# Moving a state-space set-up out of the first projection and into the first MLP of a three-layer network on one core

## The reference, cut to what matters

```python
def first_block(...):                       # layers 0 and 1
    h = concatenate([meta, x])              # 528 x 1024
    for i in range(2):
        hn = rmsnorm(h, norm_attn[i])
        h = h + (even_mixer if i == 0 else odd_mixer)(hn, ...)
        h = h + (relu(rmsnorm(h, norm_mlp[i]) @ w_up[i]) ** 2) @ w_down[i]

def even_mixer(h, ...):
    qa, ka, va, qb, kb, vb = split(h @ w_in)         # 18 tiles of 128 columns
    oa = differential attention(qa, ka, va, bias = table[bucket(k - q)])
    qb, kb = rmsnorm(qb), rmsnorm(kb)                # per head of 64
    qb, kb = axial_rope(qb), axial_rope(kb)
    ob = dense attention(qb, kb, vb)
    return concat(oa, ob) @ w_out

def odd_mixer(h, ...):                               # window of 128, bias by the same table, a sink column
    ...

def s5_ssm(u, a, log_dt, b, c, d_skip):              # in layer 2, which also has attention and an FFN
    dt = exp(log_dt); bar = exp(a * dt)              # complex, 32 groups x 64 states
    bb = (bar - 1) / a * b                           # 32 x 64 x 16
    h_t = bar * h_(t-1) + bb @ u_t ; y_t = Re(c @ h_t) + d_skip * u_t
```

## Time and profile before

| | us |
|---|---|
| time, median of 3 runs (2389.45 to 2392.06) | 2391.89 |
| the profiled execution, its own time | 2387.33 |
| its span | 2385.5 |
| PE busy | 2218.0 (93%) |
| PE weight loads busy | 1864.6 (78%) |
| DVE, ACT, POOL busy | 1173.1 (49%), 785.0 (33%), 884.8 (37%) |

### The profile page before, as it was taken

One profiled execution on the slowest core, in us unless ns is written; L12 is line 12 of the kernel. 1 busy time (PEld: TensorE's weight loads), 2 busy tenths in 40 slices (PEclk: granted clock), 3 DMA queues, 4 the chain that ended last, 5 costly groups with the idle time before them and its releaser, 6 DMA issues.

```text
span 2385.5 us, 33836 instructions
## 1 busy us (share of the span) xinstructions
PE 2218.0 (93%) x13234; PEld 1864.6 (78%) x13234; DVE 1173.1 (49%) x1732; ACT 785.0 (33%) x1271; POOL 884.8 (37%) x384
## 2 busy tenths in 40 slices
PE   3596979999999999999999998999999999999996
PEld 2595757999999976787888877778867788887875
DVE  4666765651253326564045346857654554443224
ACT  2122655331222236432122323234332332222223
POOL 0231024444444434444444433323333444444442
PEclk9797989999999999999999999999989999999998
DMA  5753000333333350133333354323222333332321
GB/s 139 144 187 68 1 1 20 90 96 89 88 95 91 88 168 2 46 96 93 92 97 90 95 141 114 115 64 91 78 73 69 93 104 90 97 92 86 97 85 54
DMA packets 371761, 209.93 MB, mean 88 GB/s; under 512 B 25935, under 2 KB 362928, under 8 KB 370752
## 3 DMA queue, kind: packets, MB, share of 16 engines
q1 hardware_dynamic: 353088, 184.21, 26.8%
q10 hardware_dynamic: 18560, 24.13, 4.4%
HBM read 196.85 MB, written 15.41 MB: 89 GB/s over the span
## 4 chain that ended last, share of the span: by engine, by line
issue 40%; PE 32%; POOL 18%; DVE 5%; ACTq 2%; ACT 2%; DMA 1%; POOLq 0%; SPq 0%; DVEq 0%
POOL w_lo L731 17%; PE acc L799 8%; PE acc L800 8%; PE acc L801 8%; PE acc L875 2%; PE ops L904 2%; ACTq L1353 2%; PE tps L893 1%; DVE probs L1929 1%; ACT probs L1370 1%; PE ops L891 1%; POOL probs L754 1%; DVE root L2269 1%; PE tps L858 0%; ACT probsT L1386 0%
## 5 line engine op out<-in xcount | busy, mean ns | idle before, releaser
L731 POOL TENSOR_TENSOR w_lo<-raw,w_hi 128x1024 fp32r<-128x1024 f32 x328 | 804.1, 2451 | 1256.1 <-ACT w_hi L1257 1241.2
L1257 ACT ACTIVATE w_hi<-raw 128x1024 fp32r<-128x1024 f32 x327 | 346.7, 1060 | 1132.5 <-PE acc L801 1064.2
L799 PE MATMUL acc<-hr_hi,w_hi 128*128 128x512 f32 x1120 | 450.2, 402 | 6.7 <-DVE u_t L2419 5.5
L800 PE MATMUL acc<-hr_lo,w_hi 128*128 128x512 f32 x1120 | 445.1, 397 | 0.0
L801 PE MATMUL acc<-hr_hi,w_lo 128*128 128x512 f32 x1120 | 445.1, 397 | 0.0
L799 PE MATMUL acc<-hn_hi,w_hi 128*128 128x264 f32 (+1 forms) x896 | 265.9, 297 | 39.2 <-POOL w_lo L731 35.0
L800 PE MATMUL acc<-hn_lo,w_hi 128*128 128x264 f32 (+1 forms) x896 | 263.2, 294 | 0.0
L801 PE MATMUL acc<-hn_hi,w_lo 128*128 128x264 f32 (+1 forms) x896 | 262.8, 293 | 0.0
L799 PEld LDWEIGHTS acc<-hr_hi,w_hi 128*128 128x128 f32 x1120 | 211.9, 189 | 63.5 <-issue 7.0
L801 PEld LDWEIGHTS acc<-hr_hi,w_lo 128*128 128x128 f32 x1120 | 211.8, 189 | 51.5
L800 PEld LDWEIGHTS acc<-hr_lo,w_hi 128*128 128x128 f32 x1120 | 212.1, 189 | 50.2 <-issue 0.7
(11 more groups left out here) (370 smaller groups left out, 3747.9 us busy)
## 6 DMA issues: line engine op xcount, KB each, us to landing
raw<-in_w_up SPq DMA_DIRECT2D x64, 512.0 KB, 4.0
raw<-in_w_down SPq DMA_DIRECT2D x64, 512.0 KB, 3.8
raw<-in_w_in SPq DMA_DIRECT2D x56, 512.0 KB, 3.8
raw<-in_w_ffn_gate SPq DMA_DIRECT2D x22, 512.0 KB, 3.8
raw<-in_w_ffn_up SPq DMA_DIRECT2D x22, 512.0 KB, 3.8
raw<-in_w_in_even SPq DMA_DIRECT2D x18, 512.0 KB, 7.6
raw<-in_w_ffn_down SPq DMA_DIRECT2D x16, 512.0 KB, 3.8
bias_c<-bias_c_d SPq DMA_DIRECT2D x1, 5392.0 KB, 17.7
```

Of the source, the lines that this page charges most:

```text
L731: nc.gpsimd.tensor_tensor(w_lo[:, part], raw[:, slot], w_hi[:, part].bitcast(F32), ALU.subtract).then_inc(sems["lo"], T.up("lo"))
L799: mm(out, w_hi[:, part, w0 + k, :], xh, start=s0, stop=False)
L800: mm(out, w_hi[:, part, w0 + k, :], xl, start=False, stop=False)
L1257: fn(w_hi[:, n % 2], raw[:, n % 4], ACT.Copy).then_inc(sems["hi"], T.up("hi"))
```

## The change

- **Start.** `x` and the meta tokens are SP's first loads; the ten small loads are issued by ACT. The squares are summed by PE with a matrix of ones (L959 of the changed file) as they come, in place of DVE's additions.
- **State-space set-up.** All of it leaves the start and `even_in`. Its loads are issued by SP in `even_out` (`ssm_loads`), after a clearing of `rows2` that DVE does behind attention B. DVE does the arithmetic in pieces, one after each tile of `up00`, `down00` and `up01` (`next(setup)`), the big products in halves of 1024 numbers; PE transposes the parameters in `up00` and does `kernel_products` and `turn_powers` in `down00`; the products by `c` overwrite `pw_re` and `pw_im`, so they wait for `turn_powers`. `up00` and `down00` are unrolled.
- **Bias tables.** ACT issues only `bias_a_d` at the start. The band part of the other table is spread by SP (`bands_d`, eight DMAs in `up00`); its 17 leading columns are made by 32 small products on PE (`lead_products`). SP loads the table in the middle of `odd_q`, in three DMAs, not after it.
- **Heads.** Order of `even_in`: the six tiles of the B part, the four of A's values, then queries and keys in turn. The norms of the heads are done after tiles 1 to 5, SP sends `rot_e` behind its load of tile 11, DVE rotates one head after each of tiles 9 to 13, and the values are transposed after tiles 6 to 10.

The products stand behind a tile's own work, never ahead of the taking of its accumulator. The diff, cut to its core:

```diff
@@ SP
-            for r0, v in ((0, a["norm_attn"]...
-                load(rows[r0:r0 + v.shape[0], :], v, "vec_in")
-            load(ident[:], a["c_ident"], "vec_in")
-            load(meta_in[:], a["meta_tokens"], "x_in")
             for t in range(4):
                 load(xin[:, t, :], a["x"][0, t * P:(t + 1) * P, :], "x_in")
+            load(meta_in[:], a["meta_tokens"], "x_in")
...
+            def spread_bands(n):
+                hs, at, w = 4 * (n // 2), (0, 3 * P)[n % 2], (3 * P, 2 * P)[n % 2]
+                load(bands_d[hs:hs + 4, :, at:at + w], bass.AP(band_d.tensor, ...), "bands_out")
...
+            def bias_c_load(first):
+                if first:
+                    T.saw("rstd", 3)
+                    sp.wait_ge(sems["rstd"], T.at("rstd"))
+                    sp.wait_ge(sems["lead_out"], T.at("lead_out"))
+                    sp.wait_ge(sems["bands_out"], T.at("bands_out"))
+                    load(lead_o[:].rearrange("p x h m -> p (x h m)"), lead_d, "bias_in")
+                at, c, w = (BAND_W, 3 * P, 2 * P) if first else (0, 0, 3 * P)
+                load(bias_c[:, :, at + LEAD_2:at + LEAD_2 + w], bands_d[:, :, c:c + w]..., "bias_in")
-            units(even_in, {3: setup_loads, 14: mixer_loads})
-            units(even_out)
+            units(even_in, {3: setup_loads, 11: swap_heads, 12: bias_a_load})
+            units(even_out, {4: ssm_loads})
-                units(by_name[f"up0{half}"])
+                units(by_name[f"up0{half}"], {} if half else {2 + n: lambda n=n: spread_bands(n) for n in range(8)})
-            units(odd_q)
-            load(bias_c[:], bias_c_d.rearrange("h p c -> p h c"), "bias_in")
+            units(odd_q, {2: lambda: bias_c_load(True), 3: lambda: bias_c_load(False)})
@@ PE
-            project(even_in, None, H_LO, first_stats, after={
-                6: kernel_products, **{7 + n: lambda n=n: turn_powers(n) for n in range(4)},
-                **{11 + n: head_sums(n) for n in range(5)}})
-            tokens_first(qkv_e, (8, 9, 10, 11, 17))
+            project(even_in, None, H_LO, None, after={
+                0: bias_products, 1: head_sums(0), 2: after_third, 3: head_sums(2), 4: head_sums(3), 5: head_sums(4),
+                **{6 + n: lambda v=v: value_tokens(v) for n, v in enumerate((17, 8, 9, 10, 11))}})
...
+                turns = {1: lambda: turn_parameters(0), 2: lambda: turn_parameters(1)}
+                tables = {2: kernel_products, **{3 + n: lambda n=n: turn_powers(n) for n in range(4)}}
+                project(by_name[f"up{i}0"], None, H_LO, (first_stats, second_stats)[i], {} if i else turns)
+                project(by_name[f"down{i}0"], None, ("hidden_lo", MLP_HALF), None, {} if i else tables)
@@ ACT
-            for at, q0, w0, w in ((0, N_META + P, P - 1, 3 * P), (BAND_W, N_META, 2 * P - 1, 2 * P)):
-                dma(bias_c_d[:, :, at:at + LEAD_2], bass.AP(bias_d.tensor, ...), "bias_c_out")
-                dma(bias_c_d[:, :, at + LEAD_2:at + LEAD_2 + w], bass.AP(band_d.tensor, ...), "bias_c_out")
@@ DVE, in mlp(0)
+                        if i == 0 and isinstance(m, int):
+                            next(setup, None)
```

More of the change, by code:

```diff
@@ new lines, in bias_products, with lead_products @@
+            def bias_products():
+                T.saw("consts", 64)
+                pe.wait_ge(sems["consts"], T.at("consts"))
+                for c in range(0, N_REL, 512):
+                    n = min(512, N_REL - c)
+                    b = open_("t_")
+                    close(mm(tps[b][0:20, 0:n], table[:], onehot[:, c:c + n], start=True, stop=True), b, "t_")
+            def lead_products():
+                T.saw("bias_rows", 2)
+                pe.wait_ge(sems["bias_rows"], T.at("bias_rows"))
+                b = open_("t_")
+                for x, q0 in enumerate((N_META + P, N_META)):
+                    for m in range(N_META):
+                        at = q0 - m - 1
+                        c = (x * N_META + m) * 16
+                        ins = mm(tps[b][:, c:c + 16], bias_back[:, at:at + P], ident[0:20, 4:20], start=True, stop=True)
+                close(ins, b, "t_")
@@ new lines, in _ @@
+                fn(hn_hi[:, k, :], h[:, k, :], ACT.Copy, scale=gains[:, k:k + 1]).then_inc(sems["h_hi"], T.up("h_hi"))
+                if k > 1:
+                    T.saw("summed")
+                    act.wait_ge(sems["summed"], T.at("summed"))
+                fn(sq[:, k % 2, :], h[:, k, :], ACT.Square).then_inc(sems["square"], T.up("square"))
+                if k == 4:
+                    T.saw("raw0", 16)
+                    act.wait_ge(sems["raw0"], T.at("raw0"))
+                    fn(w_hi[:, 0], raw[:, 0], ACT.Copy).then_inc(sems["hi"], T.up("hi"))
@@ L1499, in _ @@
[L1499 to L1506 removed]
+                if m == 0:
+                    for _ in range(3):
+                        others(T, "t_")
+                if m == 1:
+                    T.saw("bias_rows", 2)
+                    act.wait_ge(sems["bias_rows"], T.at("bias_rows"))
+                    dma(bias_d, bias_row[:], "bias_out")
+                    dma(band_d, band_row[:], "bias_out")
@@ L1547, in _ @@
+            mlp(0, parameters, tables, store_ca)
+            act.wait_ge(sems["ssm_out"], T.at("ssm_out"))
             project(odd_kv, first=first_stats)
```

659 lines of the change are left out of this document (371 added, 288 removed).

## The result

| | before | after |
|---|---|---|
| time, median (range, 4 runs each) | 2390.67 (2388.72 to 2392.06) | 2347.01 (2346.19 to 2351.95) |
| profiled execution, own time; its span | 2387.33; 2385.5 | 2347.00; 2345.1 |
| ratio after / before, 95% interval | | 0.9822 [0.9805, 0.9839] |
| PE busy; mean granted clock | 2218.0; 0.967 | 2232.4; 0.974 |

The account below looks back on a forecast made before the run. PE bounds the kernel except in two nearly idle stretches, up to 79.3 and 230.7 us. Terms: 80.5 + 2 - 15.1 - 1 - 2 = 64.4 us gained, giving 2327.5 against the median 2391.9; range 2315 to 2345.

Parts of the forecast that it names:

- the chain behind the last tile: After even_in's last tile at 204.6: heads normed, rot_e sent, five heads rotated, first attention A scores only at 230.70.
- Slower and no change: Slower, 0.01: PE stays at its lower level after kernel_products; no change, within some 5 us: 0.01.
- The start: Before even_in: x issued first, h copies from about 10.4 us, first even_in product at 29.5, bounds 27.5 and 33.
- lead_products: In even_in: 32 small products on PE, taken at 4.6 us, bounds 3.6 and 5.3.
- The set-up on DVE lies beside PE: In up00 and down00: DVE's set-up hides, up to 4 us behind where PE's next accumulator has 5.8.
- set-up is not hidden: Rival, up00 to up01: 14 units with large products each lose 1.5 us, 21 in all, so 2348; chance 0.12.
- The danger on POOL: In the MLP: DVE products lengthen POOL's w_lo to up to 3.6 us; cost 1, bounds 0 and 6.
- kernel_products: In the MLP: 10.6 us added on PE, part of 15.1 together with turn_powers and parameter transposes.
- Bands on SP: In up00: 5.24 MB on SP between weight loads, against three units of reserve; cost nothing, bound 8.
- odd_q: In odd_q: bias_c between the weight loads makes unit 4 arrive late; 2 us lost, bounds 0 and 6.
- Attention: After the first scores: PE that hasn't stood and an exponential table already loaded gain 2 us, bounds 1 and 3.
- Heads within the projection: In even_in: ACT and DVE keep pace with head norms, and rot_e's DMAs hold SP 6.7 us; both cost nothing.

Follow-up runs that it names:

- run 11: The kernel before, with the four bias_c_d DMAs issued by SP behind its fourth load of even_out, not by ACT at the start: 2359.1 us, 0.9878.
- Run 8: The changed kernel with the identity as SP's first load and bias_c loaded behind all loads of odd_q: 2341.3 us, 0.9789 to the kernel before.
- run 9: The changed kernel with all 64 kernel_products reading rows 0 to 63 instead of alternating halves: 2364.3 us, 0.9879 to the kernel before.
- runs 10 and 11: The kernel before with bias_c_d's DMAs issued by SP: first behind its even_in loads, 2366.0 us; then behind its fourth even_out load, 2359.1 us.
- run 12: The changed kernel with leading columns by DMA, bias_c behind odd_q's loads, kernel_products in four groups and the set-up laid out anew: 2313.3 us, 0.9670.
- run 4: The changed kernel with the last seven set-up pieces of up00 moved to down00 and kernel_products after tile 4: 2342.9 us, 0.9790 to the kernel before.

## Why the prediction was wrong

- **What bounds the kernel** was read rightly: the two idle stretches are gone, and run 11 shows ACT's issues as the cause of the first (25.8 us by themselves). That the chain behind the last tile was worth its 24.0 is read from the two traces; no run has it alone. Slower and no change were far off.
- **The start**: the first product of `even_in` at 30.2 (29.5 forecast). The copies began at 12.61, not 10.4: PE waited until 10.19 for the identity. Run 8 only passed that wait to another small load, so why they land so late stays open. 0.7 us. ACT prepared the second unit's weights at 29.3, not at 27. Behind the last tile it took 2.1 us; the forecast took 2.5 for terms that add to 2.2.
- **`lead_products`, the step that failed most in `even_in`**: "they cost 10.64 over a tile, 0.17 each [...] I take 4.6, bounds 3.6 and 5.3". They cost 12.2. The nearest row was the wrong one in two ways: its products cost half of these at full clock (run 9), and "half of them may not reach" the low clock was a hope; they reached it for 10.2 us. This term is 7.6 of the 8.5 missing at the first scores; the rest is the start and small excesses of the first two tiles.
- **"The set-up on DVE lies beside PE [...] it falls up to 4 us behind, and PE's next accumulator has 5.8"**: the step that failed in `up00`, where 12.3 us were lost for 2.0, the largest miss of all. The accumulator was one reserve of two, and the smaller loss (2.3 us). The other was ACT's order, `mid_hi` of a tile ahead of `w_hi` of a later one (4.7), and neither was filled again, since `w_lo` then holds DVE for 2.2 us more a tile. From tile 9 on 9.6 us were lost: 7.1 of PE idle and about 2 of half clock behind it. The rival "set-up is not hidden" (0.12) had the place and 21 us, by 14 units that lose 1.5 each; it was six tiles in one stretch. The first nine tiles lost 2.7, 1.0 forecast for the transposes and 1.5 a wait of PE for DVE's copy ahead of them.
- **The danger on POOL** (1 us, bounds 0 and 6) pointed at the right pair of engines in the wrong direction. In the first nine tiles of `up00` no `w_lo` lasted over 2.85 us; DVE's operations were the ones held. Only the last two, beside the big products, took 3.05 and 3.35.
- **`kernel_products`** 10.6: mis-sized, 13.8, all of the difference half clock. The row that it was taken from was one draw: in runs 10 and 11, which have the products where the kernel before has them, that tile took 18.06 and 18.05 for 16.44, so 12.3. With `turn_powers` (0.9 each, as forecast) `down00` lost 18.0 for 14.1; the last 0.6 is that `up01`'s first tile was taken late.
- **The move of the set-up itself** did not pay as the change makes it. It freed about 18 us in `even_in` (an estimate from the trace before: 10.6 and 3.5 of PE's own, 4.2 of waits for DVE) and cost 30.3 in `up00` and `down00`; in run 12, by the same stages and `up01`, 13.5. The forecast had 15.1 and 1 for it. No run has this move alone.
- **Bands on SP** 0: right, one wait of ACT of 3.9 us in `up00` that PE didn't see. **`odd_q`** 2: 2.9 here and 1.7 to 4.6 in the eight others, so rather too low; run 8 gives 2.5 back. **Attention** 2: 2.1, partly luck, since from 223.6 to 227.3 us were measured for it in seven kernels with the same program there. **Heads within the projection** at no cost: right, tiles with a head's norm last 6.67 to 6.69 and those in which DVE rotates a head 6.35 or 5.80, PE's own work, and PE waits for nothing in `even_in`.
- The last 0.8 us, behind attention C, I can't assign; that part of the program took 1496.3 to 1507.6 us in kernels that don't differ in it.

## What to carry to other kernels

Ask of a moved piece not only whether the engine has the time, but what stands behind that engine's output in the next engine's order: here 4 us of lateness on DVE turned the order of two of ACT's copies and fed itself. Price a run of narrow products from one that reads the same rows in the same alternation, from more than one trace, and expect it to cost the clock of the work behind it as well; where the data can be had by a DMA in a quiet stretch, do that. Work that must hide beside a tile is laid out by the tile's remainder: one product of 1.2 us in each tile of 5.8 was nearly free (0.4 us of waits in run 12), six in one tile weren't (4.3 us in run 4).
